# Weights as the stationary operand: a four-layer decoder trunk whose FFN columns and stick-breaking queries and keys are projected already turned

## What is computed

```python
D_MODEL, SEQ, DEPTH, D_FF = 1024, 256, 4, 2816
def _swiglu(x, w_in, w_out):
    gate, up = jnp.split(x @ w_in, 2, axis=-1)
    return (jax.nn.silu(gate) * up) @ w_out

def _sb_mixer(x, w_in, w_out):
    h = (x @ w_in).reshape(bsz, S, 3, 16, 64)
    o = _stick_breaking(h[:, :, 0], h[:, :, 1], h[:, :, 2])
    return o.reshape(bsz, S, 1024) @ w_out
...
for i in range(DEPTH):
    x = layernorm(a * x + 0.5 * _swiglu(x, ffn1_w_in[i], ffn1_w_out[i]))
    x = layernorm(a * x + mixer[i % 3](x))
    x = layernorm(a * x + 0.5 * _swiglu(x, ffn2_w_in[i], ffn2_w_out[i]))
    x = x + sigmoid(x @ ple_w_gate[i]) * (p[i] @ ple_w_proj[i])
```

## Time and profile before

| | |
|---|---|
| median of 3 runs | 2258.08 us (2257.26 to 2260.7) |
| profiled execution | 2257.6 us, span of its records 2255.5 us |
| TensorE matmuls | 2223.3 us busy, 99% of the span, 10756 instructions |
| TensorE weight loads | 1823.4 us, 81%, 10756 |
| VectorE | 1324.5 us, 59% |
| ScalarE | 1084.1 us, 48% |
| transfers | 401.4 MB, 178 GB/s, 54.3% of 16 engines' span |

### The profile page before, as it was taken

The page is one execution under the profiler, slowest core; times in us unless marked ns, Lnnn a source line. Parts: engine busy times, 40 slices in busy tenths (PEclk is TensorE's granted clock), DMA queues, the critical chain, the costliest instruction groups (busy, mean ns, idle before and its releaser), DMA issues.

```text
span 2255.5 us, 26355 instructions
## 1 busy us (share of the span) xinstructions
PE 2223.3 (99%) x10756; PEld 1823.4 (81%) x10756; DVE 1324.5 (59%) x1598; ACT 1084.1 (48%) x1340; POOL 18.0 (1%) x53
## 2 busy tenths in 40 slices
PE   8999999999999899999999999999999999999999
PEld 7888878888888678888888878878888888888887
DVE  5446575456545864556446766765456545666546
ACT  5444564445444654445444453454445444565433
POOL 0000000000000000000000000000000000000000
PEclk9999999999999999999999999999999999999999
DMA  8654546555654365647564544546555654546552
GB/s 294 193 179 151 175 133 207 189 186 185 207 186 150 131 203 180 198 134 236 187 200 144 174 142 140 178 127 210 186 191 178 209 191 150 168 150 205 178 188 105
DMA packets 212936, 401.44 MB, mean 178 GB/s; under 512 B 12368, under 2 KB 30928, under 8 KB 212688
## 3 DMA queue, kind: packets, MB, share of 16 engines
q1 hardware_dynamic: 212816, 399.76, 54.3%
HBM read 398.66 MB, written 1.05 MB: 177 GB/s over the span
## 4 chain that ended last, share of the span: by engine, by line
PE 89%; DVE 6%; ACT 2%; DMA 2%; issue 1%; POOL 0%; SPq 0%; ACTq 0%; DVEq 0%; POOLq 0%
PE ps L1110 26%; PE ps L1112 26%; PE ps L1111 26%; PE ps L1153 4%; DVE wl L775 2%; PE ps L1218 1%; PE ps L1217 1%; PE ps L1216 1%; ACT wh L501 1%; DMA raw<-in_ple_w_gate 1%; PE ps L1338 1%; PE ps L1441 1%; PE ps L1357 1%; DMA raw<-in_sb_w_in 0%; ACT arena L553 0%
## 5 line engine op out<-in xcount | busy, mean ns | idle before, releaser
L775 DVE TENSOR_TENSOR wl<-raw,wh 128x1024 fp32r<-128x1024 f32 x730 | 867.2, 1222 | 482.4 <-ACT wh L501 478.1
L501 ACT ACTIVATE wh<-raw 128x1024 fp32r<-128x1024 f32 x730 | 752.3, 1058 | 592.3 <-PE ps L1112 413.5
L1110 PE MATMUL ps<-wh,xh 128*128 128x512 f32 x2064 | 813.7, 394 | 4.7 <-DVE xl L782 4.7
L1112 PE MATMUL ps<-wh,xl 128*128 128x512 f32 x2064 | 804.4, 390 | 0.0
L1111 PE MATMUL ps<-wl,xh 128*128 128x512 f32 x2064 | 803.8, 389 | 0.0
L1110 PEld LDWEIGHTS ps<-wh,xh 128*128 128x128 f32 x2064 | 388.7, 188 | 86.0 <-DVE xl L782 6.4
L1112 PEld LDWEIGHTS ps<-wh,xl 128*128 128x128 f32 x2064 | 388.3, 188 | 81.0
L1111 PEld LDWEIGHTS ps<-wl,xh 128*128 128x128 f32 x2064 | 388.9, 188 | 76.7
L1110 PE MATMUL ps<-wh,hth 128*128 128x512 f32 x736 | 289.5, 393 | 0.0
L1112 PE MATMUL ps<-wh,htl 128*128 128x512 f32 x736 | 287.1, 390 | 0.0
L1111 PE MATMUL ps<-wl,hth 128*128 128x512 f32 x736 | 286.7, 390 | 0.0
(11 more groups left out here) (108 smaller groups left out, 1111.0 us busy)
## 6 DMA issues: line engine op xcount, KB each, us to landing
raw<-in_ffn_w_in SPq DMA_DIRECT2D x352, 512.0 KB, 4.6
raw<-in_ffn_w_out SPq DMA_DIRECT2D x176, 512.0 KB, 4.5
raw<-in_dil_w_in SPq DMA_DIRECT2D x72, 512.0 KB, 4.3
raw<-in_sb_w_in SPq DMA_DIRECT2D x48, 512.0 KB, 4.7
raw<-in_ple_w_gate SPq DMA_DIRECT2D x32, 512.0 KB, 4.8
raw<-in_sb_w_out SPq DMA_DIRECT2D x16, 512.0 KB, 5.2
gb<-in_ln_g SPq DMA_DIRECT2D x12, 512.0 KB, 6.6
gb<-in_ln_b SPq DMA_DIRECT2D x12, 512.0 KB, 7.3
```

The source lines that it names most:

```text
L501: act.activation(wh[:, u % RING, :], raw[:, u % RAWS, :], ACT.Copy).then_inc(hi_done, 1)
L775: dve.tensor_tensor(wl[:, u % RING, :], raw[:, u % RAWS, :], wh[:, u % RING, :].bitcast(F32), ALU.subtract).then_inc(lo_done, 1)
L1110: pe.matmul(out_, a_h, b_h, start=start, stop=False)
L1112: return pe.matmul(out_, a_l, b_h, start=False, stop=stop)
```

## The change

- **FFN.** Block 0 stays as it was, but its transposes come after one unit of the next gate columns and go to banks 4 and 5. The other 2304 columns of each half run in nine sub-blocks of 256 (`SUB`): two units gate, two units up, and, two sub-blocks long after, two units down. Their units hold four row blocks of 256 columns (1 KB rows). `by_column` makes the weight piece (128 inputs x 128 columns) stationary. Moving are the activations of all 256 tokens: against the high weights high and low side by side (512 columns, from the new joint buffer `xhl`), against the low weights the high ones alone (256 columns), added onto the first half of the bank. VectorE sums the two halves of the bank (`tensor_reduce`, new: `gate_sum`, and in `hidden`), ScalarE takes the SiLU in SBUF, VectorE multiplies, ScalarE rounds (`hidden_hi`), VectorE forms the rest (`hidden_lo`). No transposes there.
- **Stick-breaking.** Values come first in the first half, then queries and keys by column in two parts of 256 columns each, `summed` by VectorE straight into `qT` and `kT`. The scale 1/8 of the queries is put into the split of their weight units (`scaled`). The filling between the steps of the heads is newly dealt out.
- `tokens`, `head_t` and `copy_t` for stick-breaking and `gate_and_up` go.

```diff
+        xhl = sb("xhl", [P, D // P, 2, NT, P], F32R)
+        xh, xl = xhl[:, :, 0], xhl[:, :, 1]
...
+def ffn_base(j):
+    return 8 * j if j < 2 else 6 * j + 4 - 2 * (j == NJ)
+def h_slot(j):
+    return 2 * ((j + 1) % 3) if j else 0
+def part_bank(what, hh, part):
+    if what == "q":
+        return 2 + 2 * part * (hh == 0)
+    return 4 + 2 * part if hh else 6 - 6 * part
...
-                    load(wout, k, c * BLK, BLK)
+                for j in range(1, NJ + 1):
+                    for col in (0, FF):
+                        for k in (0, 4):
+                            load(win, k, BLK + (j - 1) * SUB + col, SUB)
+                    if j == 1:
+                        down(0), down(2)
+                    elif j < NJ - 1:
+                        down(2 * j)
+                down(2 * NJ - 2)
+                down(2 * NJ, 2 * NJ + 2)
...
-                    act.activation(wh[:, u % RING, :], raw[:, u % RAWS, :], ACT.Copy).then_inc(hi_done, 1)
+                    act.activation(wh[:, u % RING, :], raw[:, u % RAWS, :], ACT.Copy,
+                                   scale=HD ** -0.5 if u in scaled else 1.0).then_inc(hi_done, 1)
+            def hidden_hi(i, j):
+                act.wait_ge(h_done.sem, h_done.at(i, j))
+                act.activation(hth[:, h_slot(j):h_slot(j) + 2].rearrange("p c t m -> p c (t m)"), hs, ACT.Copy).then_inc(th_done.sem, 1)
+            def silu(i, j):
+                if j:
+                    act.wait_ge(gs_done.sem, gs_done.at(i, j))
+                    ins = act.activation(gs, gs, ACT.Silu)
...
+                    if u in scaled:
+                        ins = dve.scalar_tensor_tensor(wl[:, u % RING, :], raw[:, u % RAWS, :], HD ** -0.5, wh[:, u % RING, :].bitcast(F32),
+                                                       ALU.mult, ALU.subtract)
+            def gate_sum(i, j):
+                dve.wait_ge(w_used, ends["gate", i, j])
+                dve.tensor_reduce(gs, ps[:, 0:2, :].rearrange("p c (r n) -> p c n r", r=2), AX.X, ALU.add).then_inc(gs_done.sem, 1)
+            def hidden(i, j):
+                dve.wait_ge(w_used, ends["up", i, j])
+                if j:
+                    own(dve.tensor_reduce(us, ps[:, 2:4, :].rearrange("p c (r n) -> p c n r", r=2), AX.X, ALU.add))
+                    dve.wait_ge(silu_done.sem, silu_done.at(i, j))
+                    ins = dve.scalar_tensor_tensor(hs, gs, 0.5, us, ALU.mult, ALU.mult)
+            def ffn(i, u0):
+                to(u0, 13)
+                hidden(i, 0)
+                to(u0, 14)
+                hidden_t(i)
+                for j in range(1, NJ + 1):
+                    b = ffn_base(j)
+                    to(u0, b + 8)
+                    gate_sum(i, j)
+                    to(u0, b + 10)
+                    hidden(i, j)
+                    to(u0, b + 10 + (j < NJ))
+                    hidden_lo(i, j)
+                to(u0, 70)
+                def summed(what, hh, part):
+                    dve.wait_ge(w_used, ends[what, i, hh, 0, part])
+                    bank = part_bank(what, hh, part)
+                    dst = (qT if what == "q" else kT)[:, 0, 2 * part:2 * part + 2, :]
+                    dve.tensor_reduce(dst, ps[:, bank:bank + 2, :].rearrange("p c (r n) -> p c n r", r=2), AX.X, ALU.add).then_inc(tok_done.sem, 1)
...
+            def by_column(half, bank):
+                u = st["u"]
+                st["u"] += 1
+                ready(u)
+                for c in range(2):
+                    for k in range(4):
+                        n = 4 * half + k
+                        w_h, w_l = (view(w, u % RING, SUB)[:, k, c * P:(c + 1) * P] for w in (wh, wl))
+                        x_h, x_hl = (xhl[:, n, 0:r].rearrange("p r t m -> p (r t m)") for r in (1, 2))
+                        if n == 0:
+                            pe.matmul(ps[:, bank + c, :], w_h, x_hl, start=True, stop=False)
+                            pe.matmul(ps[:, bank + c, 0:SUB], w_l, x_h, start=False, stop=False)
+                        else:
+                            pe.matmul(ps[:, bank + c, 0:SUB], w_l, x_h, start=False, stop=False)
+                            ins = pe.matmul(ps[:, bank + c, :], w_h, x_hl, start=False, stop=n == 7)
+                ins.then_inc(w_used, 1)
+                for j in range(1, NJ + 1):
+                    if j == 1:
+                        pe.wait_ge(silu_done.sem, silu_done.at(i, 0))
+                    else:
+                        pe.wait_ge(gs_done.sem, gs_done.at(i, j - 1))
+                    by_column(0, 0)
+                    if j == 1:
+                        hidden_t(i)
+                    by_column(1, 0)
+                    pe.wait_ge(h_done.sem, h_done.at(i, j - 1))
+                    by_column(0, 2)
+                    by_column(1, 2)
+                    if j < NJ - 1:
+                        down(j - 1)
...
+                        run(v, True, before=opening(i, 2))
+                        for what, part in (("q", 0), ("q", 1), ("k", 0)):
+                            by_column(0, part_bank(what, 0, part))
+                            by_column(1, part_bank(what, 0, part))
+                        pe.wait_ge(v_done.sem, v_done.at(i, 0, 0))
+                        by_column(0, part_bank("k", 0, 1))
...
                     z(hh, 0)
+                    z(hh, 1)
                     if hh == 0:
+                        by_column(1, part_bank("k", 0, 1))
+                        by_column(0, part_bank("q", 1, 0))
+                        by_column(1, part_bank("q", 1, 0))
+                        pe.wait_ge(tok_done.sem, tok_done.at("k", i, 0, 0, 1))
+                    else:
+                        run(v[1:4], False)
                     cum(hh, 0)
                     cum(hh, 1)
```

More of the change, by code:

```diff
@@ L44 @@
 BLK = 512
-NJ = FF // BLK
+SUB = 256
+NJ = (FF - BLK) // SUB
 SW = 3 * P + 2
@@ L89, in steps_of @@
         else:
-            steps += [("q", hh, 0), ("k", hh, 0), ("v", hh, 0), ("attn", hh, 0)]
+            steps += [(what, hh, 0) for what in ("qkv" if hh else "vqk")] + [("attn", hh, 0)]
     return steps
@@ L314, in build_program @@
                         ends[what, i, hh, g] = at
-                        if what != "v":
+                        if what != "v" and mixer_of(l) == "sb":
+                            for part in range(2):
+                                ends[what, i, hh, g, part] = at - 2 + 2 * part
+                                tok_done.note(what, i, hh, g, part)
+                            if what == "q":
+                                scaled.update(range(at - 4, at))
+                        elif what != "v":
                             tok_done.note(what, i, hh, g)
                             th_done.note(what, i, hh, g)
-                            if mixer_of(l) == "sb":
-                                t_ready.note(what, i, hh, g)
                         if what in ("v", "kv"):
@@ L443, in _ @@
                             col = g * 3 * D + "qkv".index(what) * D + hh * BLK
-                            for k in range(0, 8, 2):
-                                load(win, k, col, BLK)
+                            if name == "sb" and what != "v":
+                                for part in range(2):
+                                    for k in (0, 4):
+                                        load(win, k, col + part * SUB, SUB)
+                            else:
+                                for k in range(0, 8, 2):
+                                    load(win, k, col, BLK)
                     norm_load(i)
@@ L1244, in ffn @@
+                down(NJ - 2)
+                pe.wait_ge(tl_done.sem, tl_done.at("h", i, NJ - 1))
+                y0 = y_items(2, hth, htl, chunk0=h_slot(NJ - 1), first=False, last=False)
+                y1 = y_items(2, hth, htl, chunk0=h_slot(NJ), first=False)
+                run([y0[0], y1[0], y0[1], y1[1]], True, y=(1, 3),
                     before=closing(i, lambda t, n: wait(pe, tl_done, "h", i, NJ) if (t, n) == (0, 1) else None))
```

247 lines of the change are left out of this document (101 added, 146 removed).

## The result

The changed kernel takes 2246.65 us (median of 5, 2245.72 to 2246.88) where the kernel before took 2257.94 beside it: the ratio is 0.9948 [0.9937, 0.9959], 11.3 us faster. The forecast was faster by 21 us, so the direction was right and the time lies in the range, but the size was forecast almost twice too large.

A forecast was written before the change was run, and what follows sets the result against it. TensorE, busy 99% of the span at full clock, was taken to bound the kernel; -39.6 us removed and +18.6 us added made -21.0, taking 2257.6 to 2236.6 us, with a range of 2228 to 2254 us.

The forecast's parts named there:

- What bounds the kernel, and how a matmul is priced: TensorE, busy 99% of the span, bounds; a matmul costs the distance between starts, 226.7 ns (512 columns) or 120.6 (256).
- What is removed: On TensorE, 352 transposes go from FFN and stick-breaking stages, 44 groups of eight at 0.90 us: 39.6 us less.
- What is added: On TensorE, 320 by-column units of 16 matmuls instead of 12, each 2.778 us, 0.058 more: 18.6 us added.
- rival 1: Long matmuls behind short ones on TensorE stay late: +57.6 us added, 2276 us; chance 0.04 in full, 0.15 for 2243 to 2253.5.
- VectorE and ScalarE: In the FFN stages their splits, reductions (1.22 us each) and products stay hidden behind TensorE's matmuls: no cost.
- Rival 2: VectorE's reductions run far slower and bind; at 4.9 us each, 180 us in all, some 2420 us; chance 0.04.
- Loads with 1 KB rows: 288 more weight loads come as 1 KB rows instead of 2 KB, yet land in time: no cost.
- The weight loads: TensorE's loading of weights, 1280 loads more on a row already at 81%, is no bound because loads overlap.
- Rival 3: The fixed 13 ns a matmul does not arise for a short one behind a long one: 2218 to 2223 us; chance 0.05.

## Why the prediction was right, and where it was off

- **What bounds the kernel, and how a matmul is priced**: held. Distances of starts, not mean durations, gave 227 and 120 ns, and runs of one width have just these with the operands exchanged.
- **What is removed** (39.6 us): 352 transposes, as counted; the price per group is supported by the doubled transposes, 0.87 us for a second group in their timeline, and by the stage without waits (0.43 us less, 0.45 by the sum).
- **What is added** (18.6 us): the step that failed. It was mis-sized, 32.0 us measured, 0.100 us a unit and not 0.058. I had the right row, the long ones 0.2325 apart behind the short ones in the earlier trace rows, and named turns as what no row shows, but took "fades within a few matmuls" for "paid once". It is paid once per change of width, and this kernel changes seven times a unit. It was rival 1 in its lower third: 0.100 lies a third of the way between the two ends that I had priced (0.058 and 0.18), and the range held because it reached there. The time fell into the stretch from 2243 to 2253.5 that had a chance of 0.15, not into the 0.66 of the forecast. Rival 1 also put a third of the lateness at 2243 us; by its own prices that is -39.6 + 31.6, so 2249.6. The upper end supposed that all of the lateness of an isolated change returns in each pair; in turns it is 6 to 7 ns instead of 15 to 19.
- **VectorE and ScalarE**: held but for one stop. Reductions 1.22 us, no wait of TensorE for a sum, a product or a split in the by-column groups, but one of 0.95 us for block 0's product in the first FFN, where I had read the cover in the second FFN alone and put the term at nothing; 67% of VectorE are busy instead of 59%. Rival 2 did not occur.
- **Loads with 1 KB rows**: held, their median to landing on the page of the changed kernel is 4.6 us for the FFN's first matrix, as before.
- **The weight loads**: 82% busy on the page after, against 81% in the earlier trace rows. The Trainium skill (Perfetto Trace Analysis, Identifying the Most-Contended Engine) advises to judge TensorE by its share of peak arithmetic and by the busy share of the weight loads, and I set the second against the earlier trace rows. The kernel with all short matmuls ran 24 loads a unit, 0.12 us apart though each lasts 0.19, with the loads busy for 88% of the span, and a matmul cost what one of 256 columns costs in the earlier trace rows, so the number of loads did not set the pace. Whether the fixed 13 ns come from changing the weights for each matmul was not tested: every kernel here does so.
- **Waits at stage ends**: left out. My sum had only what the change says it does. The changed kernel has 4.2 us less of them, more than a third of the result; that the splits moved in front of a wait did it is inferred from the kernel with two splits forward. The terms that I had missed (+13.4, -4.2 and +0.95) make 10.1 us, and I missed by 9.7. That the miss was not larger is luck: without the shorter waits the same unit price would have left about 7 us of gain, a third of the forecast.
- **Rival 3** (the fixed 13 ns vanish behind a long one) is out: it had 0 to 5 us added, and 32.0 were.

## What to carry to other kernels

Price a matmul by the distance of two starts in a run like the one that you are going to have, and if none has its pattern, count how often the pattern changes and charge each change. Where matmuls of different widths are needed in one accumulation, group them by width, and let neighbouring groups meet at the same width: here the order of the same instructions was worth 13.4 us, more than the 11.3 of the change itself. And look at what stands on VectorE in front of a stage's end: a split that waits for its load there delays the norm that TensorE needs next.

## What the runs showed of the hardware

With fresh weights for every matmul, one of 512 columns takes 227 ns from start to start and one of 256 columns 120 ns in runs of its own width, whichever operand is stationary: 13 ns beyond the columns at 2.4 GHz in both cases. A change from short to long costs 15 to 19 ns on top if it stands alone and 6 to 7 if the widths take turns, in one PSUM bank or in two. What causes it was not found; the runs exclude the bank, and the stationary operand as a price of its own. That the transposes, which are short too, are followed by late matmuls in the earlier trace rows fits it. A second group of eight transposes directly behind the first costs 0.87 us. A reduction of 1024 elements from PSUM to 512 takes 1.22 us, as the copy of 1024 does.
